# Attention values with the values held still, two groups of heads side by side, and exponentials divided before they are turned

## The chip, the cores and the metric

The kernel runs on one core of a Trainium2 chip. The metric is the device time of one launch in microseconds (us); the time before is the median of three runs. A profile is one further execution of the same kernel, with a span (first to last instruction) and a time of its own.

## What is computed

Two layers over 256 tokens of width 1024. Each layer has a mixer and then a feed-forward part: layer 0 a dense SwiGLU, layer 1 a top-2-of-8 expert SwiGLU; a last RMSNorm ends it. The change lies in the attention half of the mixers:

```python
scores = einsum('bnqkgd,bnskd->bnkgqs', qb, kb) * (HEAD_DIM ** -0.5)   # 8 query heads, 2 key/value heads, head_dim 64
m = maximum(max(where(valid, scores, NEG_INF)), sink_b)
p = exp(scores - m)
denom = sum(p) + exp(sink_b - m)
out = einsum('bnkgqs,bnskd->bnqkgd', p / denom, vb)
y_att = rmsnorm(out, att_out_g);  y_conv = rmsnorm(short_conv(bg, cg, u, conv_w), conv_out_g)
return concatenate([y_att, y_conv], axis=-1) @ w_out
```

With 256 tokens every query block of 128 sees both key blocks, so a head has 128x256 scores for each of the two query tiles (t = 0 and 1). Query heads 0 to 3 use the first key/value head, 4 to 7 the second.

## The kernel before

The order of each engine's work is written out by hand; the engines meet only at semaphores, and each works through its own queue in order. Line numbers are those of the profile.

**Weights in pieces.** The projections run at full float32 accuracy by splitting both sides in a high and a low part. A weight piece is 128x1024: ScalarE copies the high part (L809), VectorE subtracts it (L1213, the low part), TensorE then does three products (L1897 to L1899) for each 128x512 output. Pieces live in a ring of 6. In a mixer they are numbered 0 to 25: q 0 to 3, kv 4 and 5, c 6 to 9, u 10 to 13, b 14 to 17, out0 18 to 21, out1 22 to 25. The loads are issued on SyncE's queue. `OUT_ORDER` makes the output projection take the four conv blocks (k = 4 to 7) first and the four attention blocks (k = 0 to 3) last.

**The attention of one tile t.** TensorE computes the scores of 8 heads in 4 banks of two heads (L1956). VectorE masks a bank (L1314), takes the row maximum (L1316) and its negative (L1317); ScalarE then makes the two exponentials of the bank with their sums (L886), after the fourth bank also that of the sink (L890). TensorE transposes the 16 blocks of exponentials (`turn_probs`, L1968) into the same banks; ScalarE and VectorE copy two banks each to `probT` (L809, L1330). `values` (L1978) holds a block of `probT` (128x128) as weights and streams 64 columns of v, 16 products for a tile, each of which is two records in the trace. VectorE divides the outcome by the denominators (`attended`, L1335).

**Around it.** The exponentials of tile 0 are turned between pieces u3 and b0; values of tile 0 come after piece b3, then `turn_probs` of tile 1, the transposes of the conv gate (L2021), values of tile 1, and the output projection. After its first piece TensorE transposes the attended values of both tiles (L2039), ScalarE and VectorE make their high and low parts (L809, L1404). VectorE's queue behind the scores of tile 1 is: the conv (L1377, L1381), `attended` of tile 0, the copies of `probT`, the product with the gate (L1391), the low parts of the conv blocks (L1396, for which ScalarE's high parts come first), the sums of squares (L1400).

Of the kernel before, what the change touches and what calls it, by code (L numbers as in the profile page):

```python
# [25 lines left out]
ALU = mybir.AluOpType  # L26
# [34 lines left out]
             ("out0", 4, 1, 2), ("out1", 4, 2, 2)]  # L61
# [269 lines left out]
CONSTS = 7  # L331
# [3 lines left out]
def build_trunk(nc, x_d, pos_d, mix_g, w_in, conv_w, sink, att_g, conv_g, w_out, ffn_g, dg, du, dd,  # L335
                router, eg, eu, ed, final_g, out_d):
    ctx = ExitStack()
    with ctx:
# [163 lines left out]
        def e_at(s, g):  # L502
# [21 lines left out]
        att = qT.rearrange("p c n -> p (c n)").rearrange("p (t n) -> p t n", t=NT)  # L524
# [4 lines left out]
        sq_sum = silu[:, 0, :]  # L529

# [23 lines left out]
        av_done, att_done, attss_done, attms_done, attstd_done, attn_done = (  # L554
            sem("av_done"), sem("att_done"), sem("attss_done"), sem("attms_done"), sem("attstd_done"), sem("attn_done"))
# [3 lines left out]
        attT_done, mixhi_done, mixlo_done = sem("attT_done"), sem("mixhi_done"), sem("mixlo_done")  # L559
# [75 lines left out]
        w_out_v = w_out.rearrange("l (h p k) n -> l h p k n", h=2, k=4)  # L635
# [10 lines left out]
        def _(sp):  # L646
# [3 lines left out]
            def mixer_loads(layer):  # L650
# [4 lines left out]
                for name, _, buf, _ in MIX_UNITS:  # L655
# [26 lines left out]
            def dense_down(j):  # L682
                if j < 2:

                    sp.wait_ge(mixlo_done, 8)
# [71 lines left out]
        def _(pool):  # L757
# [13 lines left out]
            nc.gpsimd.dma_start(g_att[:, :, :], att_g.rearrange("l (p k) -> p l k", k=4)).then_inc(consts_in, 16)  # L771
# [26 lines left out]

            nc.gpsimd.dma_start(rout[:, :, 0:NE], router[0].rearrange("(k p) e -> p k e", k=KT)).then_inc(router_in, 16)
# [7 lines left out]
        def _(act):  # L807
# [73 lines left out]
            def exps(layer, t):  # L881
# [7 lines left out]
                act.wait_ge(sinkd_done, 2 * layer + t + 1)  # L889
                nc.scalar.activation(esink[:, t, :], sinkd[:, t, :], ACT.Exp).then_inc(exp_done, 1)  # L890

            def probT_copy(layer, t):
                act.wait_ge(probT_done, 2 * layer + t + 1)
                for b in range(2):
                    copy(probT[:, b * 512:(b + 1) * 512], bank[b][:, :]).then_inc(probT_out_a, 1)

            def mixer(layer):
# [53 lines left out]
                act.wait_ge(yc_done, layer + 1)  # L951
                for k in range(CT):
                    copy(act_hi[:, 4 + k, :], yc[:, k, :], scale=g_conv[:, layer, k:k + 1]).then_inc(mixhi_done, 1)
                nc.scalar.activation(sq, yc, ACT.Square).then_inc(sq_done, 1)
                nc.scalar.activation(table_warm[:, :], eps[:, :], ACT.Sqrt)
                pieces(22, 24)
                for t in range(NT):
                    act.wait_ge(att_done, 2 * layer + t + 1)
                    nc.scalar.activation(prob[:, t * 512:(t + 1) * 512],
                                         att[:, t, :], ACT.Square,  # L960
                                         accum_out=ss_a[:, t:t + 1]).then_inc(attss_done, 1)
                act.wait_ge(attT_done, layer + 1)
                for k in range(4):
                    copy(act_hi[:, k, :], bank[k // 2][:, (k % 2) * 256:(k % 2) * 256 + 256],
                         scale=g_att[:, layer, k:k + 1]).then_inc(mixhi_done, 1)
                act.wait_ge(attss_done, 2 * (layer + 1))
                nc.scalar.activation(std_a[:, :], ss_a[:, :], ACT.Sqrt, bias=eps[:, 0:1],
                                     scale=1.0 / AW).then_inc(attstd_done, 1)
                act.wait_ge(cms_done, layer + 1)
                nc.scalar.activation(std_c[:, :], bank[CMS][:, 0:NT], ACT.Sqrt, bias=eps[:, 0:1],  # L970
# [223 lines left out]
        def _(dve):  # L1194
# [110 lines left out]

            def masked_scores(layer, t):
# [12 lines left out]
                dve.wait_ge(masked_done, 4 * (i + 1))  # L1319
                v.tensor_tensor(sinkd[:, t, :], sink_sb[:, layer, :], nmx[:, t, :], ALU.add).then_inc(sinkd_done, 1)  # L1320

            def denominators(layer, t):
                dve.wait_ge(exp_done, (NH + 1) * (2 * layer + t + 1))
                link(v.tensor_tensor(den[:, t, :], psums[:, t, :], esink[:, t, :], ALU.add))
                v.reciprocal(rden[:, t, :], den[:, t, :]).then_inc(rden_done, 1)

            def probT_copy(layer, t):
                dve.wait_ge(probT_done, 2 * layer + t + 1)
# [3 lines left out]
            def attended(layer, t):  # L1332
                dve.wait_ge(av_done, 2 * layer + t + 1)
                dve.wait_ge(rden_done, 2 * layer + t + 1)
                v.tensor_tensor(att[:, t, :].rearrange("p (h d) -> p h d", h=NH),  # L1335
                                bank[6 + t][:, :].rearrange("p (h d) -> p h d", h=NH),
# [1193 lines left out]
```

## Time and profile before

| what | value |
|---|---|
| median of 3 runs | 1269.55 us (1269.49 to 1270.73) |
| profiled execution, its own time | 1270.25 us |
| its span | 1268.5 us |
| TensorE busy | 1241.0 us (98%) |
| VectorE busy | 579.1 us (46%) |
| ScalarE busy | 435.6 us (34%) |
| granted TensorE clock, mean | 0.996 |

The difference of 1.75 us between span and time lies around the span. The first mixer lies between 0 and about 104 us, the dense part up to 292 us, the second mixer up to about 391 us, the experts after that. TensorE's busy time is modelled, since matmuls overlap: what an operation costs in a row is read from the start of one row to the start of the next.

### The profile page before, as it was taken

Reading aid. Unit: us, or ns where it says so; the run is one execution under the profiler, and the core shown is the slowest. Engines: PE = TensorE matmul, PEld = TensorE weight load, DVE = VectorE, ACT = ScalarE, POOL = GpSimd, SP = SyncE. Lnnn points to the kernel's source line nnn. Section 1 sums busy time; section 2 is a strip of 40 time slices with the busy share of each in tenths; the row PEclk is TensorE's granted clock in tenths of the full one; section 3 lists DMA queues with packets and bytes.
Section 4 is the critical chain, followed back from the end, with each engine's and each line's share of the span. In section 5 each row is a group of like instructions: output and inputs, shape, how many; then the busy total and the mean of one; then the engine's idle time right before and its main releaser. Section 6 shows DMA issues by size and latency. Waiting matters only on the chain.

```text
span 1268.5 us, 31549 instructions
## 1 busy us (share of the span) xinstructions
PE 1241.0 (98%) x14347; PEld 966.9 (76%) x14347; DVE 579.1 (46%) x944; ACT 435.6 (34%) x678; POOL 11.8 (1%) x35
## 2 busy tenths in 40 slices
PE   7999999999998999999999999999999999999997
PEld 6888888888887677777767778766677778768894
DVE  5786555556687556565765656421100112210003
ACT  6664444446554454354643545200000000000002
POOL 3000000000000000000000000000000000000000
PEclk9999999999998999999999999999999999999999
DMA  9345844165005999999999999999999999999993
GB/s 345 139 154 221 315 161 172 70 234 195 5 1 218 420 421 426 419 421 420 421 425 421 420 421 420 422 423 419 420 414 421 397 397 399 413 419 421 423 421 133
DMA packets 109018, 419.50 MB, mean 331 GB/s; under 512 B 4632, under 2 KB 8768, under 8 KB 100688
## 3 DMA queue, kind: packets, MB, share of 16 engines
q1 hardware_dynamic: 107776, 416.30, 81.0%
q8 instruction: 115, 1.88, 0.5%
q0 software_dynamic: 544, 1.12, 0.3%
q14 instruction: 23, 0.19, 0.0%
q10 hardware_dynamic: 560, 0.01, 0.0%
HBM read 416.37 MB, written 1.05 MB: 329 GB/s over the span
## 4 chain that ended last, share of the span: by engine, by line
PE 85%; DMA 11%; DVE 2%; ACT 1%; SPq 1%; issue 1%; DVEq 0%; ACTq 0%
PE bank L2281 25%; PE bank L1897 13%; PE bank L1898 13%; PE bank L1899 13%; PE bank L2345 12%; DMA ring<-in_moe_w_down 6%; DMA ring_after<-in_moe_w_down 2%; DMA ring<-in_moe_w_up 2%; PE bank L2216 2%; PE bank L2210 2%; PE bank L1978 1%; ACT w_hi L809 1%; SPq L723 1%; PE bank L1956 1%; DVE w_lo L1668 1%; PE bank L1968 1%
## 5 line engine op out<-in xcount | busy, mean ns | idle before, releaser
L1668 DVE TENSOR_TENSOR w_lo<-ring,w_hi 128x896 fp32r<-128x896 f32 (+2 forms) x192 | 202.1, 1089 | 80.3 <-ACT w_hi L809 74.5
L2281 PE MATMUL bank<-ring,late_acts 128*32 128x224 f32 x4736 | 234.0, 353 | 0.0
L2281 PEld LDWEIGHTS bank<-ring,late_acts 128*32 128x32 f32 x4736 | 188.9, 110 | 40.9 <-issue 5.0
L809 ACT ACTIVATE w_hi<-ring 128x896 fp32r<-128x896 f32 (+2 forms) x192 | 176.0, 948 | 117.7 <-PE bank L1899 72.8
L1083 ACT ACTIVATE silu_buf<-bank 128x224 f32<-128x224 f32 (+2 forms) x76 | 29.2, 395 | 433.9 <-PE bank L2281 433.9
L1897 PE MATMUL bank<-hi,act_hi 128*128 128x512 f32 (+1 forms) x400 | 155.3, 388 | 0.8 <-DVE lo L1213 0.8
L1899 PE MATMUL bank<-hi,act_lo 128*128 128x512 f32 (+1 forms) x400 | 153.2, 383 | 0.0
L1898 PE MATMUL bank<-lo,act_hi 128*128 128x512 f32 (+1 forms) x400 | 153.2, 383 | 0.0
L1213 DVE TENSOR_TENSOR lo<-raw_gu,hi 128x1024 fp32r<-128x1024 f32 x96 | 113.5, 1222 | 39.9 <-ACT hi L809 39.6
L1691 DVE TENSOR_TENSOR silu_buf<-silu_buf,bank 128x224 f32<-128x224 f32 (+2 forms) x76 | 32.0, 435 | 207.3 <-PE bank L2281 186.0
L809 ACT ACTIVATE hi<-raw_gu 128x1024 fp32r<-128x1024 f32 x96 | 97.5, 1061 | 40.4 <-PE bank L1899 35.7
L2281 PE MATMUL bank<-ring,first_acts 128*32 128x224 f32 x2048 | 104.3, 354 | 0.6 <-ACT silu_buf L1083 0.6
L1897 PE MATMUL bank<-w_hi,wide_hi 128*128 128x512 f32 (+1 forms) x256 | 94.9, 371 | 0.9 <-ACT silu_buf L1083 0.8
L1898 PE MATMUL bank<-w_lo,wide_hi 128*128 128x512 f32 (+1 forms) x256 | 94.0, 367 | 0.0
L1899 PE MATMUL bank<-w_hi,wide_lo 128*128 128x512 f32 (+1 forms) x256 | 93.8, 366 | 0.0
L2345 PE MATMUL bank<-ring,at_buf 128*32 128x256 f32 x1456 | 85.8, 380 | 3.3 <-DMA ring<-in_moe_w_down 3.3
L2281 PEld LDWEIGHTS bank<-ring,first_acts 128*32 128x32 f32 x2048 | 63.6, 110 | 33.0 <-issue 5.1
L1897 PEld LDWEIGHTS bank<-hi,act_hi 128*128 128x128 f32 x400 | 75.8, 190 | 16.1 <-DVE lo L1213 1.2
L1899 PEld LDWEIGHTS bank<-hi,act_lo 128*128 128x128 f32 x400 | 75.6, 189 | 14.9
L1898 PEld LDWEIGHTS bank<-lo,act_hi 128*128 128x128 f32 x400 | 75.9, 190 | 14.0
L2345 PEld LDWEIGHTS bank<-ring,at_buf 128*32 128x32 f32 x1456 | 51.5, 110 | 33.5 <-DMA ring<-in_moe_w_down 4.7
L1897 PEld LDWEIGHTS bank<-w_hi,wide_hi 128*128 128x128 f32 x256 | 48.0, 188 | 10.9 <-DVE w_lo L1668 3.1
(257 smaller groups left out, 1340.2 us busy)
## 6 DMA issues: line engine op xcount, KB each, us to landing
ring<-in_moe_w_up SPq DMA_DIRECT2D x59, 1792.0 KB, 20.3
ring<-in_moe_w_gate SPq DMA_DIRECT2D x58, 1792.0 KB, 20.2
ring<-in_moe_w_down SPq DMA_DIRECT2D x53, 1792.0 KB, 20.4
ring_after<-in_moe_w_down SPq DMA_DIRECT2D x11, 1792.0 KB, 19.7
raw_gu<-in_w_in SPq DMA_DIRECT2D x7, 2048.0 KB, 12.3
raw_gu<-in_dense_w_gate SPq DMA_DIRECT2D x5, 2048.0 KB, 7.9
raw_gu<-in_dense_w_up SPq DMA_DIRECT2D x5, 2048.0 KB, 12.5
raw_d<-in_dense_w_down SPq DMA_DIRECT2D x5, 2048.0 KB, 14.5
```

The costliest lines, as they stand in the source:

```text
L809: return nc.scalar.activation(out, in_, ACT.Copy, **kw)
L1083: nc.scalar.activation(out, gate, ACT.Silu).then_inc(e_silu_done, 1)
L1213: v.tensor_tensor(out, src, h, ALU.subtract).then_inc(lo_done, 1)
L1668: v.tensor_tensor(w_lo[:, n % WP, 0:b - a], flat(u)[:, a:b], w_hi[:, n % WP, 0:b - a], ALU.subtract).then_inc(w_lo_done, 1)
L1691: v.tensor_tensor(gated_e, gated_e, up, ALU.mult).then_inc(e_gated_done, 1)
L1897: mm(out, ah, wh, start=start, stop=False, **kw)
L1898: mm(out, ah, wl, start=False, stop=False, **kw)
L1899: return mm(out, al, wh, start=False, stop=stop, **kw)
L2210: ins = mm(bank[b][:, i * m:(i + 1) * m], xn[:, t, k * P:(k + 1) * P], sel[:, t, 0:m], start=t == 0, stop=t == 1)
L2216: return mm(bank[b][:, :], gselT[0:m, tile, t * P:(t + 1) * P], yt[0:m, tile, c * 512:(c + 1) * 512], start=start, stop=stop)
L2281: ins = mm(bank[b][32 * c:32 * c + 32, 0:n], acts[STEPS[s][0]][:, k, g.col:g.col + 32], w[:, c], start=k == 0, stop=k == KT - 1)
L2345: ins = mm(bank[g.acc][32 * c:32 * c + 32, g.acc_col:g.acc_col + 256], e_at(s, g)[:, 32 * f:32 * f + 32], flat(u)[:, at:at + 256], start=o ...
```

## The change

`values` swaps the roles: 64 columns of v are held as weights and the transposed probabilities of four heads (128x512) are streamed, one key/value head to output partitions 0 to 63 and the other to 64 to 127. That is 4 products a tile in place of 16. Their output has the head dimension on the partitions already, so the transposes of the attended values go, and so does the division by denominators on it; the rows of w_out and of the gain are loaded in the matching order. The division moves ahead: VectorE multiplies each head's exponentials in place by the reciprocal denominator, in two batches of four heads within `masked_scores`, each behind the score bank that follows. `turn_probs` now waits for these (`probs_done`). Tile 0 is turned one piece later, behind b0. The four copies of `probT` of tile 1 are all ScalarE's. The high and low parts of attention are made tile by tile right from the banks of `values`; the sum of squares goes over the partitions with two further small products. In the diff `denominators`, `masked_scores` and `attended` are VectorE's, `probT_copy` is ScalarE's (VectorE's own is called for tile 0 only), the functions from `turn_probs` on are TensorE's, and the last piece is of SyncE's loads.

```diff
+            def denominators(layer, t, c):
+                i = 2 * (2 * layer + t) + c
+                dve.wait_ge(exp_done, 5 * (i + 1))
+                link(v.tensor_tensor(batch(den, t, c), batch(psums, t, c), batch(esink, t, c), ALU.add))
+                link(v.reciprocal(batch(rden, t, c), batch(den, t, c)))
+                for b in SCORE_BANKS[2 * c:2 * c + 2]:
+                    for h in (2 * b, 2 * b + 1):
+                        own = prob[:, h * SEQ:(h + 1) * SEQ]
+                        v.tensor_scalar(own, own, rden[:, t, h:h + 1], None, ALU.mult).then_inc(probs_done, 1)
...
             def masked_scores(layer, t):
...
+                    if n % 2 == 1:
+                        c = n // 2
+                        dve.wait_ge(masked_done, 4 * i + n + 1)
+                        v.tensor_tensor(batch(sinkd, t, c), batch(sink_sb, layer, c), batch(nmx, t, c),
+                                        ALU.add).then_inc(sinkd_done, 1)
+                    if n >= 2:
+                        denominators(layer, t, n - 2)
...
+            def attended(layer, t):
...
+                dve.wait_ge(attss_done, i + 1)
+                for k in range(4):
+                    v.scalar_tensor_tensor(out=act_lo[:, k, tt], in0=bank[6 + t][:, k * P:(k + 1) * P],
+                                           scalar=g_att[:, layer, k:k + 1], in1=act_hi[:, k, tt],
+                                           op0=ALU.mult, op1=ALU.subtract).then_inc(attlo_done, 1)
+                v.tensor_reduce(asq_sum[:, tt], prob[:, t * 512:(t + 1) * 512].rearrange("p (k q) -> p q k", k=4),
+                                AX, ALU.add).then_inc(asq_summed, 1)
...
             def probT_copy(layer, t):
                 act.wait_ge(probT_done, 2 * layer + t + 1)
-                for b in range(2):
+                for b in range(2 if t == 0 else 4):
                     copy(probT[:, b * 512:(b + 1) * 512], bank[b][:, :]).then_inc(probT_out_a, 1)
...
             def turn_probs(layer, t):
                 for n, b in enumerate(SCORE_BANKS):
-                    pe.wait_ge(exp_done, (NH + 1) * (2 * layer + t) + 2 * n + 2)
+                    pe.wait_ge(probs_done, NH * (2 * layer + t) + 2 * n + 2)
...
             def values(layer, t):
-                for h in range(NH):
-                    g = AW + KVW + HD * (h // (NH // NKV))
-                    for kt in range(NT):
-                        ins = mm(bank[6 + t][:, h * HD:(h + 1) * HD], probT[:, h * 256 + kt * P:h * 256 + kt * P + P],
-                                 qkv[:, kt, g:g + HD], start=kt == 0, stop=kt == 1)
+                for kt in range(NT):
+                    for g in range(NKV):
+                        c = AW + KVW + HD * g
+                        four = probT[:, 1024 * g:1024 * g + 1024].rearrange("p (h k q) -> p k h q", h=4, k=NT)
+                        ins = mm(bank[6 + t][HD * g:HD * g + HD, :], qkv[:, kt, c:c + HD], four[:, kt],
+                                 start=kt == 0, stop=kt == 1)
...
                 scores(layer, 0)
                 mix_pieces(layer, "u", (6, 7), 2, 4)
-                turn_probs(layer, 0)
                 pe.wait_ge(c_out, 2 * (layer + 1))
-                mix_pieces(layer, "b", (4, 5), 0, 2)
+                mix_pieces(layer, "b", (4, 5), 0, 1)
+                turn_probs(layer, 0)
+                mix_pieces(layer, "b", (4, 5), 1, 2)
...
                 values(layer, 1)
-                out_pieces(layer, 0, 0, 1)
-                pe.wait_ge(att_done, 2 * (layer + 1))
-                for k in range(4):
-                    for t in range(NT):
-                        c = (k % 2) * 256 + t * P
-                        ins = tr(bank[k // 2][:, c:c + P], att[:, t, k:AW:4], ident[:, :])
-                ins.then_inc(attT_done, 1)
-                out_pieces(layer, 0, 1, 2)
+                out_pieces(layer, 0, 0, 3)
...
+                pe.wait_ge(asq_summed, 2 * (layer + 1))
...
-                out_pieces(layer, 0, 2, 4)
+                out_pieces(layer, 0, 3, 4)
...
-                        for h in range(2):
-                            sp.dma_start(unit[buf][:, 4 * h:4 * h + 4, :],
-                                         w_out_v[layer, h, :, :, c * 512:(c + 1) * 512]).then_inc(unit_in[buf], 16)
+                        cc = slice(c * 512, (c + 1) * 512)
+                        sp.dma_start(unit[buf][:, 4:8, :], w_out_conv[layer, :, :, cc]).then_inc(unit_in[buf], 16)
+                        for g in range(NKV):
+                            sp.dma_start(unit[buf][HD * g:HD * g + HD, 0:4, :], w_out_att[layer, g, :, :, cc])\
+                                .then_inc(unit_in[buf], 16)
```

VectorE, tile 1 of the first mixer, before (`bank` holds scores, `mx` and `nmx` their maxima, `den` and `rden` the denominators of tile 0, `y` the conv):

```order
L1324 TENSOR_TENSOR den<-psums,esink 128x8
L1325 RECIPROCAL rden<-den 128x8
L1213 TENSOR_TENSOR lo<-raw_gu,hi 128x1024 x4
L1314 TENSOR_TENSOR bank<-bank,mask 128x2x128
...
L1320 TENSOR_TENSOR sinkd<-sink_sb,nmx 128x8
L1377 TENSOR_SCALAR y<-raw_d,cw 128x256 x4
L1381 SCALAR_TENSOR_TENSOR y<-raw_d,cw,y 128x256 x8
L1335 TENSOR_TENSOR raw_d<-bank,rden 128x512
L1330 COPY raw_d<-bank 128x512 x2
L1324 TENSOR_TENSOR den<-psums,esink 128x8
L1325 RECIPROCAL rden<-den 128x8
L1391 TENSOR_TENSOR y<-y,bank 128x512 x2
```

The same stretch of VectorE's queue now, from the third score bank of tile 1 on:

```order
L1327 TENSOR_TENSOR den<-psums,esink 128x2x2
L1328 RECIPROCAL rden<-den 128x2x2
L1332 TENSOR_SCALAR raw_d<-raw_d,rden 128x256 x4
L1342 TENSOR_TENSOR bank<-bank,mask 128x2x128
L1344 TENSOR_REDUCE mx<-bank 128x2
L1345 SCALAR_TENSOR_TENSOR nmx<-mx,nsink 128x2
L1350 TENSOR_TENSOR sinkd<-sink_sb,nmx 128x2x2
L1327 TENSOR_TENSOR den<-psums,esink 128x2x2
L1328 RECIPROCAL rden<-den 128x2x2
L1332 TENSOR_SCALAR raw_d<-raw_d,rden 128x256 x4
L1409 TENSOR_SCALAR y<-raw_d,cw 128x256 x4
L1413 SCALAR_TENSOR_TENSOR y<-raw_d,cw,y 128x256 x8
```

The denominators came behind the conv and the copies; they, with eight multiplications on the exponentials (`raw_d`), now stand among the score banks and ahead of the conv.

TensorE, from the values of tile 0 on, before:

```order
L1978 MATMUL bank<-raw_d 128x64 x16
L1968 MATMUL bank<-ident,raw_d 128x128 x16
L2021 MATMUL bank<-ident,xn 128x128 x8
L1978 MATMUL bank<-raw_d 128x64 x16
L1897 MATMUL bank<-hi,act_hi 128x512
```

And the same place now:

```order
L2008 MATMUL bank<-raw_d 64x512 x4
L1998 MATMUL bank<-ident,raw_d 128x128 x16
L2052 MATMUL bank<-ident,xn 128x128 x8
L2008 MATMUL bank<-raw_d 64x512 x4
L1920 MATMUL bank<-hi,act_hi 128x512
```

The order is the same; the values have 4 products of 512 columns for 16 of 64.

## Rows read from the trace of the kernel before

**Rows 1.** Timeline of TensorE: start us, us, line, output and inputs, count [idle before].

```profile
61.77 2.00 PE L1956 MATMUL bank<-raw_d 64*128 64x256 f32 x16
...
70.25 3.68 PE L1978 MATMUL bank<-raw_d 128*128 128x64 f32 x32
73.77 1.92 PE L1968 MATMUL bank<-ident,raw_d 128*128 128x128 f32 x16
...
77.16 3.75 PE L1978 MATMUL bank<-raw_d 128*128 128x64 f32 x32 [0.51 <-DVE raw_d L1330]
80.72 0.48 PE L1897 MATMUL bank<-hi,act_hi 128*128 128x512 f32 x1
...
83.58 1.12 PE L2039 MATMUL bank<-ident,raw_d 128*128 128x128 f32 x8
84.45 0.48 PE L1897 MATMUL bank<-hi,act_hi 128*128 128x512 f32 x1
...
87.29 0.50 PE L2046 MATMUL bank<-ones,silu 128*128 128x1 f32 x4
```

**Rows 2.** Timeline of VectorE, both mixers.

```profile
48.09 0.43 DVE L1314 TENSOR_TENSOR bank<-bank,mask 128x256 f32<-128x256 f32 x1 [2.05 <-PE bank L1956]
...
49.36 0.42 DVE L1314 TENSOR_TENSOR bank<-bank,mask 128x256 f32<-128x256 f32 x1
...
53.08 0.16 DVE L1317 SCALAR_TENSOR_TENSOR nmx<-mx,nsink 128x2 f32<-128x2 f32 x1
...
55.38 2.36 DVE L1213 TENSOR_TENSOR lo<-raw_gu,hi 128x1024 fp32r<-128x1024 f32 x2 [1.93 <-ACT hi L809]
...
60.17 0.16 DVE L1324 TENSOR_TENSOR den<-psums,esink 128x8 f32<-128x8 f32 x1
...
60.48 4.58 DVE L1213 TENSOR_TENSOR lo<-raw_gu,hi 128x1024 fp32r<-128x1024 f32 x4
64.98 0.42 DVE L1314 TENSOR_TENSOR bank<-bank,mask 128x256 f32<-128x256 f32 x1
...
70.23 1.14 DVE L1377 TENSOR_SCALAR y<-raw_d,cw 128x256 f32<-128x256 f32 x4
...
77.24 1.24 DVE L1391 TENSOR_TENSOR y<-y,bank 128x512 f32<-128x512 f32 x2
79.14 1.68 DVE L1396 SCALAR_TENSOR_TENSOR act_lo<-y,g_conv,act_hi 128x256 fp32r<-128x256 f32 x4 [0.66 <-ACT act_hi L809]
...
81.56 2.01 DVE L1400 TENSOR_REDUCE silu<-gated 128x256 f32<-128x1024 f32 x1
...
105.20 0.61 DVE L1239 SCALAR_TENSOR_TENSOR act_lo<-bank,g_ffn,act_hi 128x128 fp32r<-128x128 f32 x2
...
346.85 0.42 DVE L1314 TENSOR_TENSOR bank<-bank,mask 128x256 f32<-128x256 f32 x1
```

**Rows 3.** Timeline of ScalarE, first mixer.

```profile
53.27 0.48 ACT L886 ACTIVATE raw_d<-bank,nmx 128x256 f32<-128x256 f32 x1 [0.24 <-DVE nmx L1317]
...
54.19 0.21 ACT L890 ACTIVATE esink<-sinkd 128x8 f32<-128x8 f32 x1
...
75.72 1.08 ACT L809 ACTIVATE raw_d<-bank 128x512 f32<-128x512 f32 x2 [3.30 <-PE bank L1968]
78.59 1.71 ACT L809 ACTIVATE act_hi<-y,g_conv 128x256 fp32r<-128x256 f32 x4 [1.78 <-DVE y L1391]
```

**Rows 4.** Timeline of SyncE's DMA queue, the loads of w_out.

```profile
21.83 11.91 SPq L666 DMA_DIRECT2D raw_gu<-in_w_out  x4
```

**Rows 5.** Timeline of TensorE in the experts, 32 output rows at a time.

```profile
431.08 1.72 PE L2281 MATMUL bank<-ring,first_acts 128*32 128x224 f32 x32
```

**Rows 6.** Stretches: us; busy PE, PEld, DVE, ACT, POOL; clock; DMA share; GB/s.

```profile
396.00:398.00 2.00, 1.34 (x4) 1.34 (x5) 1.83 (x12) 0.00 (x0) 0.00 (x0) 0.50 0.93 268
398.00:400.00 2.00, 2.00 (x7) 2.00 (x7) 0.64 (x3) 0.37 (x2) 0.00 (x0) 0.50 1.04 403
400.00:402.00 2.00, 2.00 (x12) 2.00 (x12) 1.38 (x2) 1.52 (x6) 0.00 (x0) 0.85 1.00 383
```

More of the change, by code:

```diff
@@ L330 @@
 FIRST_BANKS = (3, 4, 6, 7)
-CONSTS = 7
+CONSTS = 6
 POOL_STEPS = 7 + NE + 5
@@ L529, in build_trunk, with batch @@
         sq_sum = silu[:, 0, :]
+        asq_sum = silu[:, 1, :]
+        def batch(a, t, c):
+            return a[:, t, :].rearrange("p (g c i) -> p c g i", g=NKV, c=2)[:, c]
         unit_in = [sem(f"unit_in{n}") for n in range(4)]
@@ L634, in build_trunk @@
         w_in_v = w_in.rearrange("l (p k) n -> l p k n", k=KT)
-        w_out_v = w_out.rearrange("l (h p k) n -> l h p k n", h=2, k=4)
+        w_out_att = w_out[:, 0:AW].rearrange("l (g k d) n -> l g d k n", g=NKV, k=4)
+        w_out_conv = w_out[:, AW:D].rearrange("l (p k) n -> l p k n", k=CT)
         dg_v = dg.rearrange("l (p k) n -> l p k n", k=KT)
@@ L797, in _ @@
             assert n == POOL_STEPS
+            for layer in range(2):
+                for g in range(NKV):
+                    nc.gpsimd.dma_start(g_att[HD * g:HD * g + HD, layer, :],
+                                        att_g[layer, 256 * g:256 * g + 256].rearrange("(k d) -> d k", k=4),
+                                        allow_slow_non_contiguous=True).then_inc(att_gain_in, 16)
             nc.gpsimd.dma_start(rout[:, :, 0:NE], router[0].rearrange("(k p) e -> p k e", k=KT)).then_inc(router_in, 16)
@@ L1318, in masked_scores, with probT_copy @@
                                            in1=nsink[:, layer, two], op0=ALU.mult, op1=ALU.min).then_inc(masked_done, 1)
[L1319 to L1328, printed above, removed]
+                    if n % 2 == 1:
+                        c = n // 2
[4 more added lines that the diff above has]
+                        denominators(layer, t, n - 2)
+            def probT_copy(layer):
+                dve.wait_ge(probT_done, 2 * layer + 1)
                 for b in range(2, 4):
@@ L1332, in attended @@
             def attended(layer, t):
[L1333 to L1336, printed above, removed]
-                                rden[:, t, :].unsqueeze(2).to_broadcast([P, NH, HD]), ALU.mult).then_inc(att_done, 1)
+                i = 2 * layer + t
+                dve.wait_ge(attss_done, i + 1)
+                tt = slice(t * P, (t + 1) * P)
+                for k in range(4):
+                    v.scalar_tensor_tensor(out=act_lo[:, k, tt], in0=bank[6 + t][:, k * P:(k + 1) * P],
[3 more added lines that the diff above has]
+                                AX, ALU.add).then_inc(asq_summed, 1)
             def mixer(layer):
@@ L1370, in mixer @@
                                            in1=z[:, t, :], op0=ALU.mult, op1=ALU.mult).then_inc(z_done, 1)
-                denominators(layer, 0)
                 pieces(18, 22)
@@ L1384, in mixer @@
                     link(ins)
-                attended(layer, 0)
-                probT_copy(layer, 1)
-                denominators(layer, 1)
                 dve.wait_ge(bT_done, layer + 1)
@@ L2044, in mixer @@
                 pe.wait_ge(sq_summed, layer + 1)
-                for t in range(NT):
-                    ins = mm(bank[CMS][:, t:t + 1], sq_sum[:, t * P:(t + 1) * P], ones[:, 0:1], start=True, stop=True)
+                pe.wait_ge(asq_summed, 2 * (layer + 1))
+                for i, sums in enumerate((sq_sum, asq_sum)):
+                    for t in range(NT):
+                        c = i * NT + t
+                        ins = mm(bank[CMS][:, c:c + 1], sums[:, t * P:(t + 1) * P], ones[:, 0:1], start=True, stop=True)
                 ins.then_inc(cms_done, 1)
-                out_pieces(layer, 0, 2, 4)
+                out_pieces(layer, 0, 3, 4)
                 pe.wait_ge(cstd_done, layer + 1)
```

84 lines of the change are left out of this document (41 added, 43 removed).

## Prediction

> **What bounds the kernel now.** I read the page's shares first, then TensorE's timeline through both mixers, then what VectorE and ScalarE do beside it. TensorE is busy 98% of the span, and in the changed part of the first mixer its one pause is 0.51 us, ahead of the values of tile 1 [rows 1]. So TensorE's own instructions are the path there. The second mixer repeats the first 281.9 us later: the masking of tile 1 starts at 346.85 for 64.98 [rows 2]. What saves TensorE time is worth its full length, as long as what TensorE waits for is ready. VectorE's slack is therefore the question. The output projection starts at 80.72; the first conv low part that it needs is started at 79.14 and takes a quarter of 1.68 us, so it is there at about 79.6 [rows 1, 2]: a slack of only 1.1 us. Upstream VectorE has one pause, 1.93 us, behind the scores of tile 0 [rows 2].
>
> **What TensorE saves.** Values of a tile cost 73.77 - 70.25 = 3.52 us and 80.72 - 77.16 = 3.56 us [rows 1]: 32 records at 0.11 us for 64 columns each. The new form has 4 products, 8 records, of 512 columns. No row has that shape, so by the nearest ones: the scores are 16 records of 256 columns, with two halves of the array at once, in 2.00 us [rows 1]; 8 records of 512 columns are the same number of columns, so about 2.0 us. In the experts 32 records of 224 columns that use a quarter of the output columns take 1.72 us [rows 5]: 7168 column steps in 1.72 us, 0.24 ns each, while the scores have 4096 in 2.00 us, 0.49 ns. With two halves side by side 4096 steps are 2.0 us; with none, twice that, 4.0 us. I take 2.0 (the scores' row is the nearest) and keep 4.0. The saving is 1.5 us a tile. The eight transposes of the attended values also go, 84.45 - 83.58 = 0.87 us, and two more products with `ones` come, about 0.3 us from the 0.50 us of four records [rows 1]. Were that all, and the 0.51 us pause too, TensorE would be 3.52 + 3.56 - 4.0 + 0.87 + 0.51 - 0.3 = 4.2 us shorter in each mixer.
>
> The Trainium skill (TensorEngine Tiling, Key Properties) says that a change of the tiling mode drains the array. The old values form has no such change and the new one has two a tile; the rows of the scores, which have it on both sides, hold that price in their 2.00 us, so my term does not grow by the rule.
>
> **What VectorE gets.** For each tile: eight multiplications of 128x256 in place and two batches of denominators. The nearest row to a multiplication is L1377, same form, same shape, SBUF to SBUF: four in 1.14 us, 0.285 each [rows 2]. The bounds: 0.42 us, the pitch of the two-input form at that shape (1.68 / 4, L1396), and 0.19 us, close to what the tiny operations take (0.16, L1324) [rows 2]. I take 0.285. A batch of denominators is 0.31 us from the row at 60.17 to 60.48, with one more completion to wait for about 0.4. A batch is 0.4 + 4 x 0.285 = 1.55 us, 3.1 us a tile.
>
> *Tile 0.* Masking a bank is 49.36 - 48.09 = 1.27 us. Three banks from 48.09 end at 52.0 (with the sink subtraction), the first batch at 53.55, the fourth bank at 54.8. From the start of the negative maximum to the end of the sink's exponential is 54.40 - 53.08 = 1.32 us [rows 2, 3], so the second batch may start at 56.1 and ends at 57.7. VectorE then does the two low parts that it started at 55.38: 2.3 us, to 60.0; the copies and z, which before filled the queue from there (55.38 + 2.3 = 57.7) to 60.17, 2.5 us, to 62.5; four low parts, 4.5 us, to 67.05. Masking of tile 1 starts there and not at 64.98: 2.1 us later. The pause of 1.93 us has hidden part of the 3.1, and the denominators that went with 0.3 the rest. TensorE isn't hurt: with b0 (2.7 us) moved ahead, it comes to the turning of tile 0 at about 57.2, and the last heads are ready at 57.8, while the first eight transposes take 0.9 us.
>
> *Tile 1.* Three banks from 67.05: 70.95. First batch: 72.5. Fourth bank: 73.8, with its negative maximum started at 73.7. Exponentials and sink: 75.0. Second batch: 75.1 to 76.7. TensorE, 1.5 us earlier after the new values, stands at `turn_probs` at 72.25, turns the first half, and waits for the second from about 73.2 to 76.2. It ends at about 77.4; before, it was 73.77 + 1.92 = 75.7 [rows 1].
>
> *Copies.* ScalarE makes all four: two took 1.08 us [rows 3], so four take 2.0, from 77.5 to 79.5. Values of tile 1 start at 79.6 for 77.16, and end at 81.6. Behind them on VectorE the conv and its gate: `attended`, copies and denominators are gone from between, so the gate comes right behind the conv: four operations of 0.285 and eight of 0.42 are 4.5 us, with the waits between them 4.6, so it starts at 76.7 + 4.6 = 81.3. Its first half is done 0.62 us later, ScalarE's high part 0.5 us after that, the low part 0.45 us on, with the hand-overs at 83.05 (before, the row at 79.14 came 1.9 us after the gate at 77.24 [rows 2]; the gate now signals by halves, which gains 0.6). The output projection starts at 83.05, not 80.72: **2.3 us later**.
>
> *After that.* TensorE has 0.87 us less (no transposes) and 0.3 more (`ones`). The third output piece needs the attention low parts of tile 1. VectorE: conv low parts to 84.4, sum of squares 2.0 us [rows 2] from 84.8 to 86.8, four low parts of tile 0 at 0.30 (L1239: two in 0.61 [rows 2]) and a reduction of half the former size, 1.0 us: 89.0; the first low part of tile 1 at about 89.2. TensorE is there at 83.05 + 5.6 = 88.6: 0.5 us of wait. Net for the mixer: 2.3 - 0.87 + 0.3 + 0.5 = 2.2 us longer.
>
> *At nothing.* The w_out loads become three where two were; they are issued from 21.83 on for 11.91 us [rows 4], and their first low part is made after 60.48 [rows 2], more than 25 us later. The gain is loaded by four small DMAs on GpSimd's queue at its start, and needed after 80 us. The dense weights wait for low parts that shift by some 2 to 5 us; they are used much later.
>
> **Sum.** 2 mixers x 2.2 = 4.4 us. Nothing behind them is tied to a fixed time: the expert loads start when the routing is known. From the profiled execution's own 1270.25 us that is 1274.65; the median of the runs lies 0.7 below that execution, so **1274.0 us** in their terms.
>
> **The range of the likeliest case.** With 0.42 us a multiplication, 8 x 0.135 = 1.1 us more stands in the chain of tile 1 and 0.9 in that of tile 0: 2 us a mixer, 1278. With 0.19, 0.095 x 16 = 1.5 less each: 1271. With values at 4.0 us, the values of tile 1 end at 83.6 and not 81.6, 0.5 us behind the low parts: 0.5 a mixer, 1275. So 1271 to 1278.
>
> **Rivals.** (A) *VectorE keeps up, TensorE's saving counts.* 2 x 4.2 = 8.4 us off: 1261. For it: TensorE is 98% busy and VectorE only 46%. Against it: the chain above would have to be 4.6 us shorter in each mixer, and most of it are rows of the same engine in order. It decides where the last heads of tile 1 are scaled before about 73 us.
>
> (B) *TensorE's clock falls in the new pauses.* In the routing TensorE had work in small bits and pauses, and ran at the lower level (1.2 GHz) until after 400 us, although it had worked without pause from about 396.7: 1.34 + 2.00 + 0.6 us of work at half speed [rows 6], so 2.0 us lost. The new pauses of 3.0, 1.3 and 1.4 us stand close together, with 4 us of work among them. One such fall in each mixer, with the output projection behind it, adds up to 2.0 each: 1278. It decides when the pause in `turn_probs` passes about 3 us. The Trainium skill (TensorE: Matmul & The Clock Gate, HAM oscillation) warns that an array left waiting by turns falls back to half rate and pays for getting back; rows 6 show such a fall, but after emptier work than here.
>
> (C) *The slower chain and the savings cancel.* If the multiplications go at 0.19, the output projection starts 2.3 - 1.5 = 0.8 us late; if the attention low parts are then there in time, 0.8 - 0.87 + 0.3 = 0.2 us is left in each mixer: 1270. For it: nothing but one row of another place stands for the multiplications. Against it: that row has their very form.
>
> (D) *The halves don't run side by side.* Then the change doesn't do what it says on TensorE; 1275, since TensorE waits for VectorE anyway.
>
> **Chances.** Likeliest case with D, 1271 to 1278: 0.60. B 0.14. A 0.12. C 0.14. A measurement here tells a difference from about 0.2%, 2.5 us. Faster by more than that is A and a little of C, 0.14; within it the rest of C and the low end of the likeliest, 0.16; slower 0.70. The range from 1268.5 to 1278.5 leaves out A and the far end of B.
>
> **What would show it.** In the profile after: a wait of TensorE in the transposes of tile 1 for VectorE's multiplications, near 3 us, in both mixers; the multiplications at 0.28 to 0.35 us; masking of tile 1 at 67; ScalarE's four copies ending near 79.5; the first output matmul at 83 and its wait put down to the low parts of the conv; values at 2.0 us. I am wrong if the masking of tile 1 starts before 66, if the scaled heads are there before TensorE asks, or if the clock leaves 1.00 in the mixers.

## The result, and the profile after

The changed kernel takes 1273.93 us (median of 9 runs, 1272.79 to 1274.71) against 1270.23 for the one before (9 runs): ratio 1.0032, interval 1.0023 to 1.0041. It is slower, by 3.7 us. The profiled span is 1272.6 us for 1268.5.

The same markers in the two traces show where the 4.1 us of span lie. The first mixer, from the first masking operation of VectorE (48.09 before, 48.48 after) to TensorE's first transposes behind the mixer (104.12, 106.64), goes from 56.03 to 58.16 us. The dense layer behind it stays at 187.90 (to 292.02 and 294.54). The second mixer, to the start of the routing (390.99, 395.52), goes from 98.97 to 100.98. So 2.13 and 2.01 us are lost in the mixers, which is the whole 4.1 us: what is left, the first masking 0.39 us later and a part behind the routing that is 0.43 us shorter, cancels. Positions below are often given from a run's first masking operation, because the profiles start at different moments (it lies between 47.52 and 48.80 us in them).

Timeline of TensorE after, first mixer (start us, us, line, output and inputs, count, idle before and its releaser), answering to rows 1:

```profile
70.73 1.94 PE L2008 MATMUL bank<-raw_d 128*64 128x512 f32 x8
72.60 1.09 PE L1998 MATMUL bank<-ident,raw_d 128*128 128x128 f32 x8
76.33 1.49 PE L1998 MATMUL bank<-ident,raw_d 128*128 128x128 f32 x8 [2.63 <-DVE raw_d L1332]
77.62 1.91 PE L2052 MATMUL bank<-ident,xn 128*128 128x128 f32 x8
79.98 2.16 PE L2008 MATMUL bank<-raw_d 128*64 128x512 f32 x8 [0.45 <-ACT raw_d L824]
83.28 0.47 PE L1920 MATMUL bank<-hi,act_hi 128*128 128x512 f32 x1 [1.15 <-DVE act_lo L1424]
```

The values of tile 0 take 1.87 us (70.73 to 72.60) where they took 3.52. But a hole of 2.63 us stands in the turning of tile 1, and a second one of 1.15 us ahead of the output projection. That starts 34.80 us behind the first masking for 32.63 [rows 1, 2].

Timeline of VectorE after, tile 1 of the same mixer, answering to rows 2:

```profile
67.26 0.43 DVE L1342 TENSOR_TENSOR bank<-bank,mask 128x256 f32<-128x256 f32 x1
...
71.66 1.14 DVE L1332 TENSOR_SCALAR raw_d<-raw_d,rden 128x256 f32<-128x256 f32 x4
...
75.24 0.17 DVE L1327 TENSOR_TENSOR den<-psums,esink 128x4 f32<-128x4 f32 x1 [0.98 <-ACT esink L906]
...
75.66 1.14 DVE L1332 TENSOR_SCALAR raw_d<-raw_d,rden 128x256 f32<-128x256 f32 x4
76.71 1.14 DVE L1409 TENSOR_SCALAR y<-raw_d,cw 128x256 f32<-128x256 f32 x4
77.88 3.38 DVE L1413 SCALAR_TENSOR_TENSOR y<-raw_d,cw,y 128x256 f32<-128x256 f32 x8
81.30 1.29 DVE L1420 TENSOR_TENSOR y<-y,bank 128x512 f32<-128x512 f32 x2
82.65 1.68 DVE L1424 SCALAR_TENSOR_TENSOR act_lo<-y,g_conv,act_hi 128x256 fp32r<-128x256 f32 x4
```

The queue is full from the masking to the low parts of the conv but for one pause behind the sink's exponential. Waits of TensorE in the two mixers (in total, times, longest):

```profile
PE bank L1998 <- DVE raw_d L1332: 5.3, 2, 2.6
PE bank L1920 <- DVE act_lo L1424: 2.0, 2, 1.1
PE bank L2008 <- ACT raw_d L824: 0.9, 2, 0.5
```

And TensorE's clock in the stretches around them (busy PE, its count, granted clock, DMA share, GB/s):

```profile
74.00:76.00 2.00, 0.00 (x0) 1.00 1.05 408
76.00:78.00 2.00, 1.67 (x10) 0.76 1.05 410
78.00:80.00 2.00, 1.55 (x10) 0.50 0.96 369
80.00:82.00 2.00, 2.00 (x8) 0.88 0.00 1
```

The clock fell to its lower level (0.50 is 1.2 GHz) behind the 2.63 us hole. The chain of the page's fourth part says the same of the whole run: VectorE's share is 8% for 2% before, TensorE's 80% for 85%. (That is how much of the chain now runs through VectorE's queue, not how much time was lost.)

### The profile page after: what moved, and what is told of

It is laid out like the page before. It is cut to its first block, busy times and chain, and to the rows that moved or that the text cites. A ratio compares the mean times of both kernels' runs of the same rounds, so it can differ in the third digit from the quotient of the medians.

```text
span 1272.6 us, 31410 instructions
## 1 busy us (share of the span) xinstructions
PE 1238.0 (97%) x14243; PEld 955.4 (75%) x14243; DVE 589.7 (46%) x992; ACT 439.0 (34%) x690; POOL 12.6 (1%) x38
## 3 DMA queue, kind: packets, MB, share of 16 engines
q8 instruction: 114, 1.87, 0.5%
## 4 chain that ended last, share of the span: by engine, by line
PE 80%; DMA 9%; DVE 8%; ACT 1%; issue 1%; SPq 0%; ACTq 0%; DVEq 0%
PE bank L2308 25%; PE bank L2372 13%; PE bank L1920 12%; PE bank L1921 12%; PE bank L1922 12%; DMA ring<-in_moe_w_down 7%; DMA ring_after<-in_moe_w_down 2%; PE bank L2243 2%; PE bank L2237 2%; DVE w_lo L1691 1%; DVE lo L1231 1%; DVE mx L1344 1%; DVE raw_d L1332 1%; DMA raw_gu<-in_w_in 1%; DVE y L1413 0%
```

## The experiments

Theory V: the order of VectorE's queue sets the start of the output projection. Against it stand theory T (TensorE's own new instructions), the clock, and later theory D (the hand-overs between the engines). Each run is told by its time, its ratio to the kernel before, and two positions from the first masking: the start of the output projection ("start", 32.63 before, 34.80 after), and the end of the first mixer ("end", 56.03 and 58.16). The second mixer is 98.97 and 100.98. Each ratio is to the kernel before as it ran beside that experiment: 1269.68 us for the first four, 1269.79 for the next four and 1269.55 for the last four, for 1270.23 in the result. So times of different groups are compared through their ratios and positions first. A position is that of one profiled execution.

**No multiplications in tile 0.**

```
 def denominators(layer, t, c):
     ...
+    if t == 0:
+        v.reciprocal(batch(rden, t, c), batch(den, t, c)).then_inc(probs_done, 4)
+        return
```

> The changed kernel without the eight multiplications of tile 0 in both mixers (the exponentials of tile 0 stay undivided; all waits stay). Theory V (VectorE's queue sets when the output projection starts): most of the 2.3 us of tile 0 is hidden, since behind it VectorE waits for the transposes of tile 0 and for ScalarE's high parts; masking of tile 1 starts about 0.7 us earlier, so about 1.3 us off in all, 1272.6. Theory T (TensorE's own instructions set the time, its waits are small change): no difference, 1273.9.

1271.89 us, ratio 1.0022 (1.0011 to 1.0034); start 34.12, end 57.46. The 2.3 us of multiplications were worth 0.7 in each mixer; without them VectorE waits 0.50 us for ScalarE and 0.88 us for TensorE's turning ahead of its copies. V's number holds: masking of tile 1 starts 18.11 us behind the first masking for 18.78.

**No multiplications in tile 1** (the same edit with `t == 1`).

> The changed kernel without the eight multiplications of tile 1 in both mixers (the exponentials of tile 1 stay undivided; all waits stay). Theory V: all eight stand in the chain to the output projection, 8 x 0.285 = 2.3 us a mixer, so 4.6 us off, 1269.3; TensorE's wait in the transposes of tile 1 falls from 2.6 to about 1.5 us. Theory T: at most the 2.6 us wait counts and what is behind it hides nothing, so under 2 us off in all, 1272 or more.

1269.37 us, ratio 0.9998 (0.9988 to 1.0007); start 32.54, end 55.89. All 2.26 us come back, and TensorE's hole shrinks by 1.71 us:

```profile
74.59 1.09 PE L2001 MATMUL bank<-ident,raw_d 128*128 128x128 f32 x8 [0.92 <-DVE rden L1329]
...
77.83 1.94 PE L2011 MATMUL bank<-raw_d 128*64 128x512 f32 x8 [1.19 <-ACT raw_d L824]
80.99 0.47 PE L1923 MATMUL bank<-hi,act_hi 128*128 128x512 f32 x1 [1.22 <-DVE act_lo L1427]
```

**The values of tile 0 made twice.**

```
-for kt in range(NT):
+for kt in [0, 1] * (2 if t == 0 else 1):
```

> The changed kernel with the products of values of tile 0 made twice (8 products for 4, same outcome), which adds about 1.9 us of TensorE ahead of the transposes of tile 1 in both mixers. Theory V: TensorE waits there for VectorE anyway, nothing changes, 1273.9 within 0.5. Theory T: 1.9 us more in each mixer, 1277.7.

1274.4 us, ratio 1.0035 (1.0022 to 1.0047); start 34.80. TensorE got 1.71 us more work (74.63 - 71.05 for 72.60 - 70.73) and the hole became 1.71 us smaller:

```profile
71.05 3.65 PE L2008 MATMUL bank<-raw_d 128*64 128x512 f32 x16
74.63 1.09 PE L1998 MATMUL bank<-ident,raw_d 128*128 128x128 f32 x8
76.65 1.18 PE L1998 MATMUL bank<-ident,raw_d 128*128 128x128 f32 x8 [0.92 <-DVE raw_d L1332]
```

T falls: what the change saves in TensorE's values of tile 0 is worth nothing.

**Work in the hole,** so that the clock stays up.

```
+if t == 1 and n == 2:
+    for _ in range(11):
+        mm(bank[7][:, :], zeros[:, 0:P], zeros[:, :], start=True, stop=True)
```

> The changed kernel with 11 products of zeros (128x512, 0.23 us each) in TensorE's pause in the transposes of tile 1, into a bank that is free there. Rival C (the fall of TensorE's clock to the lower level behind that pause costs time): the clock stays at the upper level, and 1 to 2 us come off in each mixer, 1270 to 1272. Theory V: the clock stays up, the transposes behind the pause take 0.9 us and not 1.3 to 1.8, but the output projection still waits for the conv's low parts at 83.3; nothing comes off, 1273.9 within 0.5.

1273.56 us, ratio 1.0033 (1.0020 to 1.0045); start 34.80, end 58.16, both as in the changed kernel. The clock stayed at 1.00 and the instructions behind got their full speed:

```profile
72.61 2.78 PE L1996 MATMUL bank<-zeros 128*128 128x512 f32 x11
75.49 1.18 PE L2001 MATMUL bank<-ident,raw_d 128*128 128x128 f32 x8
76.51 1.13 PE L2055 MATMUL bank<-ident,xn 128*128 128x128 f32 x8
78.83 1.94 PE L2011 MATMUL bank<-raw_d 128*64 128x512 f32 x8 [1.19 <-ACT raw_d L824]
82.44 0.47 PE L1920 MATMUL bank<-hi,act_hi 128*128 128x512 f32 x1 [1.68 <-DVE act_lo L1424]
```

(The fall of the clock, rival C of this expectation, is rival B of the prediction.) What they gained, 1.3 us, stands in the two waits, 1.19 for 0.45 and 1.68 for 1.15. In the changed kernel the fall of the clock costs nothing.

**All four copies of tile 0 on ScalarE.**

```
-for b in range(2 if t == 0 else 4):        # ScalarE, behind turn_probs
+for b in range(4):
...
-    probT_copy(layer)                      # VectorE
```

> The changed kernel with all four copies of probT of tile 0 on ScalarE, which idles there; VectorE loses two copies of 0.6 us ahead of the masking of tile 1. Theory V (the queue of VectorE sets the start of the output projection): masking of tile 1 and all behind it 1.2 us earlier in each mixer, 2.4 us off, 1271.5. Theory D (what limits is the number of engine hand-overs, exponentials to sums to transposes to copies, not how much VectorE has in its queue): the hand-overs are the same, no difference, 1273.9.

1273.46 us, ratio 1.0031 (1.0020 to 1.0041); start 34.64. A miss: 0.16 us instead of 1.2, close to the number of theory D. VectorE got its time back and spent it waiting, since ScalarE's copies had pushed its high parts back:

```profile
59.75 1.40 DVE L1396 SCALAR_TENSOR_TENSOR xn<-bank,rstd,xn 128x512 f32<-128x512 f32 x2
62.11 4.63 DVE L1231 TENSOR_TENSOR lo<-raw_gu,hi 128x1024 fp32r<-128x1024 f32 x4 [0.96 <-ACT hi L824]
```

**And the conv's first tap on ScalarE too.**

```
+for k in range(CT):                        # ScalarE
+    copy(yc[:, k, :], zT[:, k, 0:SEQ], scale=cw[:, layer, 0, k:k + 1]).then_inc(tap_done, 1)
...
-for k in range(CT):                        # VectorE
-    ins = v.tensor_scalar(yc[:, k, :], zT[:, k, 0:SEQ], cw[:, layer, 0, k:k + 1], None, ALU.mult)
-link(ins)
+dve.wait_ge(tap_done, CT * (layer + 1))
```

> b1, and the first tap of the conv (four multiplications of 128x256, 1.14 us) from VectorE to ScalarE, ahead of the exponentials of tile 1. Theory V: another 1.1 us earlier at the gate, the output projection starts 2.3 us earlier than in the changed kernel, 4.6 us off in all, 1269.3, about the kernel before. Theory D: the attention's chain is as long as in b1 or 0.4 longer, since the exponentials of the first bank wait for the taps: no better than b1.

1271.04 us, ratio 1.0011 (1.0001 to 1.0020); start 33.49, end 56.84. The tap itself gave its 1.15 us in each mixer, where theory D had nothing. The time is still 1.7 us above the 1269.3 expected, for what the copies had not brought is missing here too. The output projection now starts with no wait, right behind the values.

**GpSimd makes half of the conv** (on the run with the copies on ScalarE; ScalarE makes the first tap of the other half).

```
+for k in (2, 3):                           # GpSimd; taps 1 and 2 likewise, then two additions
+    ins = nc.gpsimd.tensor_scalar(yc[:, k, :], zT[:, k, 0:SEQ], cw[:, layer, 0, k:k + 1], None, ALU.mult)
```

> b1, with the conv of the last two channel blocks wholly on GpSimd and the first tap of the first two on ScalarE. VectorE keeps four operations of 0.42 of the twelve. Theory V: its part of the gate could start 2.8 us earlier than in b1, but then the values of tile 1 are what ends last (masking of tile 1 is no earlier than in b1): they end about 80.8 on the scale of the changed kernel's profile, so the projection starts 2.5 us earlier than there; 5 to 5.5 us off, 1268.6. Theory D: as b1.

1275.18 us, ratio 1.0039 (1.0025 to 1.0053); start 34.71. A miss by 6.6 us. The profile explains only part of it: the profiled execution was the shortest of the five (1272.95 us, the longest 1275.92), and in it the mixers take 57.58 and 100.43 us, some 0.6 us less each than in the changed kernel, where about 2.6 was expected. What made the other executions longer is in no profile. First the timeline of GpSimd, then that of VectorE beside it:

```profile
66.51 2.28 POOL L822 TENSOR_SCALAR y<-raw_d,cw 128x256 f32<-128x256 f32 x2 [53.18 <-ACT raw_d L849]
68.89 3.77 POOL L828 TENSOR_SCALAR gated<-raw_d,cw 128x256 f32<-128x256 f32 x4
72.74 2.94 POOL L835 TENSOR_TENSOR y<-y,gated 128x256 f32<-128x256 f32 x4
```

```profile
71.50 2.11 DVE L1363 TENSOR_SCALAR raw_d<-raw_d,rden 128x256 f32<-128x256 f32 x4
73.53 0.42 DVE L1373 TENSOR_TENSOR bank<-bank,mask 128x256 f32<-128x256 f32 x1
...
75.05 0.65 DVE L1381 TENSOR_TENSOR sinkd<-sink_sb,nmx 128x4 f32<-128x4 f32 x1
76.20 0.16 DVE L1358 TENSOR_TENSOR den<-psums,esink 128x4 f32<-128x4 f32 x1 [0.50 <-ACT esink L931]
...
76.61 1.14 DVE L1363 TENSOR_SCALAR raw_d<-raw_d,rden 128x256 f32<-128x256 f32 x4
```

The four multiplications that ran beside GpSimd took 2.11 us, those behind it 1.14. They are on the chain that feeds the hole, which is 2.96 us here; so is the sink's subtraction (`sinkd`), 0.65 for 0.16.

**Two of w_out's low parts moved behind the conv's** (on the run above).

```
-pieces(18, 22)                             # ahead of tile 1's masking
+pieces(18, 20)
...
+pieces(20, 21)                             # behind act_lo of the conv
...
-pieces(22, 24)
+pieces(21, 24)                             # behind `attended`
```

> g1, with the low parts of pieces 20 and 21 (the third and fourth of out0) moved behind the conv's low parts on VectorE: masking of tile 1 starts 2.3 us earlier again. Theory V: values of tile 1 end about 2 us earlier than in g1, the projection starts 4.5 us earlier than in the changed kernel, and about 1 us comes back as a wait in the third piece, where the attention's low parts and piece 20 are late: 3.5 to 4 us a mixer, 7 to 8 off, 1266.5, faster than both kernels. Theory D: the attention's chain is set by its hand-overs; masking early doesn't help, as g1.

1273.5 us, ratio 1.0031 (1.0020 to 1.0042), a miss by 7 us. The start moved to 32.89, 1.9 us earlier than in the changed kernel where 4.5 were expected, but the mixer's end is at 58.86. The loads of the dense gate and up weights wait for 22 low parts. SyncE issued them at 89.50 and 90.11, for 67.37 and 67.98 in the changed kernel, and ScalarE sat without its pieces:

```profile
102.61 2.01 ACT L849 ACTIVATE hi<-raw_gu 128x1024 fp32r<-128x1024 f32 x2 [9.75 <-issue]
```

VectorE's low parts of them stand ahead of its update of `x`, for which TensorE then waited 2.50 us. The dense layer took 189.31 us for 187.90. The second mixer, which has no dense layer behind it, took 98.22 us, 2.8 less than in the changed kernel.

These two misses changed several things at once. The last four runs leave GpSimd out and take the rest apart; what GpSimd's share costs in time was not tried by itself.

**The first tap alone on ScalarE** (copies two and two as in the changed kernel).

> The changed kernel, but ScalarE makes the convolution's first tap (four copies of 128x512 with a scale) beside its other work, in place of VectorE's four multiplications of 128x512 by the tap, 0.28 us each, 1.14 us in all, in each of the two mixers; the four copies of the probabilities stay two and two. Theory V (VectorE's queue sets the output projection's start): masking of tile 1 comes no earlier, but the low parts of the convolution come 1.14 us earlier, and the output projection starts just as the values of tile 1 end, about 1.1 us earlier: 1273.9 - 2 x 1.14 = 1271.6 us. Theory D (the hand-overs between TensorE, ScalarE and VectorE set it, not the sum of VectorE's work): no change, 1273.9 us.

1271.83 us, ratio 1.0015 (1.0006 to 1.0024). The time is the one expected from V, but not in the way expected: start 34.80, unmoved, end 57.65, and the second mixer 99.76. So 0.51 us came in the first mixer, where the third output piece no longer waits for the attention's low parts, and 1.22 in the second. The TensorE rows of the first say why, with its clock at 0.66, 0.50, 0.50 and 0.63 in the four stretches from 74 to 82 us:

```profile
75.37 1.97 PE L2002 MATMUL bank<-ident,raw_d 128*128 128x128 f32 x8 [2.62 <-DVE raw_d L1338]
77.13 1.91 PE L2056 MATMUL bank<-ident,xn 128*128 128x128 f32 x8
79.49 2.90 PE L2012 MATMUL bank<-raw_d 128*64 128x512 f32 x8 [0.45 <-ACT raw_d L825]
82.32 0.50 PE L1924 MATMUL bank<-hi,act_hi 128*128 128x512 f32 x1
```

In the second mixer the clock stayed at 1.00 behind a hole of the same length, and the same values took 1.94; the output projection started 33.54 us behind that mixer's first masking, for 34.72 in the changed kernel. In the first the wait for the low parts of the conv is gone, so the slow clock is on the path: it ate 0.7 us of the mixer.

**Two low parts later, the loads kept in their places.**

```
+# first tap on ScalarE, pieces(18, 20), (20, 21), (21, 24) as above
 # SyncE, loads of the dense gate (w = 0) and up (w = 1)
-sp.wait_ge(lo_done, base + [MIX_FIRST["out1"], MIX_PIECES][j])
+sp.wait_ge(lo_done, base + [MIX_FIRST["out0"], MIX_PIECES][j])
...
+if j == 0 and w == 1:
+    sp.wait_ge(lo_done, base + MIX_FIRST["out1"])
```

> The kernel with the first tap on ScalarE, and on VectorE the low parts of two of the output projection's four weight pieces moved behind the low parts of the convolution's result, one of them behind those of the attention. The load of the dense gate's weights no longer waits for all 22 low parts but for the first of the output projection's, the load of the up weights for the later ones, so that both keep their places in time. Theory V: about 2.3 us of low parts leave the way of the masking of tile 1 in each mixer; the output projection then waits for the values instead; my sum gives 2.5 us less for each mixer than in the changed kernel: about 1269 us. Theory D: 1271.6 us or more. If the order of two loads matters, as in the run before this one where they were issued 22 us later, this one must not show ScalarE waiting 9.8 us for the dense pieces.

1270.71 us, ratio 1.0004 (0.9995 to 1.0013); start 32.55, end 56.42, second mixer 99.28. The start came 2.25 us earlier; the mixer gained only 1.7, for the time is 1.7 us above what I expected. The attention's low parts, ahead of which one of the two moved ones now stands, are waited for 1.7 us over both mixers. The loads did not quite keep their places: the gate's was issued at 59.88 us, for 67.37 in the changed kernel, and the up load at 89.91. The late one did no harm, since the gate's was early.

**The attention's low parts ahead of the sums of squares.**

```
-dve.wait_ge(attss_done, i + 1)             # `attended`
+dve.wait_ge(atthi_done, i + 1)
...
+# ScalarE: high parts of both tiles, then sq, then both Squares behind attlo_done
+# VectorE: attended 0, 1; then the reduction of sq, then those of the attention
```

> The kernel before this one, and behind the convolution the low parts of the attention's values of both tiles come ahead of the sums of squares of both (ScalarE makes the high parts of both tiles first and the squares after, VectorE reduces the squares last). The waits of TensorE for those low parts (2.0 us of waits over two mixers for the first, 0.5 us for the second) go. Theory V: another 1 us for each mixer: about 1267 us, less than the kernel before the change. Theory D: as the run above, 1269 us or more; the reductions that now come last would be waited for at the end of the mixer.

1269.09 us, ratio 0.9993 (0.9984 to 1.0002); start 32.54, end 55.67, second mixer 98.50. This is 4.8 us less than the changed kernel and the best of those that do the whole work. It cannot be told from the kernel before. In its two mixers, by the profile, it is 0.4 and 0.5 us shorter than that. I expected 1267; over the run above the mixers gained 0.75 and 0.78 us for 1 each, and the rest of the miss is that run's own. The time by itself would fit theory D (1269 or more); what D cannot explain is the start, 2.26 us earlier, and the gain of the tap. What TensorE still waits for in both:

```profile
PE bank L2014 <- DVE raw_d L1343: 3.1, 2, 1.6
PE bank L2024 <- ACT raw_d L827: 2.4, 2, 1.2
PE bank L1936 <- DVE act_lo L1437: 0.9, 2, 0.5
```

**The same with the old trigger of the loads.**

> The kernel above with the loads of the dense gate's and up's weights behind all 22 low parts again. The two theories on the stall of the run with moved pieces: if it was the late trigger, the loads are issued some 20 us later again, ScalarE waits about 9.8 us for the first dense piece in the first mixer and TensorE 2.5 us at its end, and the time is about 2.5 us above the kernel above, 1269.5 us; if it was GpSimd's share of the convolution, which is absent here, the time is the same as that of the kernel above.

1275.05 us, ratio 1.0043 (1.0029 to 1.0056). The start is 32.55, as in the run above, but the first mixer ends at 60.41, 4.7 us later. First TensorE's rows there, then ScalarE's, then SyncE's queue:

```profile
107.99 0.49 PE L1906 MATMUL bank<-ident,x 128*128 128x128 f32 x2 [4.58 <-DVE x L1452]
108.31 1.28 PE L1894 MATMUL bank<-ident,x 128*128 128x128 f32 x6
```

```profile
103.82 2.00 ACT L825 ACTIVATE hi<-raw_gu 128x1024 fp32r<-128x1024 f32 x2 [11.98 <-issue]
```

```profile
89.48 0.56 SPq L710 DMA_DIRECT2D raw_gu<-in_dense_w_gate  x1
90.09 0.67 SPq L710 DMA_DIRECT2D raw_gu<-in_dense_w_up  x1
```

The trigger was the cause of the stall, not GpSimd. The size I expected, 2.5 us, was too small: TensorE asked 0.5 us earlier than in the run with GpSimd (55.83 us behind the first masking for 56.36), and ScalarE had its pieces 1.5 us later than there (56.24 for 54.70). Behind the wait the clock fell (0.63 and 0.51 from 108 to 112 us), and the dense layer took 189.42 us and not 187.90. The second mixer, 98.47, is as in the run above.

## Why the prediction was right

The mechanism was right, and the number, 1274.0 for 1273.93, came for the most part by its own steps:

- *VectorE gets 16 more multiplications a mixer, at 0.285 us.* They took 1.14 us for each four, as the conv's row said. The two runs without them give what each half is worth: 0.7 us in tile 0 and 2.26 in tile 1. The guess that part of tile 0's is hidden was right.
- *Masking of tile 1 at 67.05, second batch at 75.1.* Less the 0.39 us by which the profile starts later, it was 66.87 and 74.85.
- *TensorE waits about 3.0 us in the turning of tile 1.* 2.63.
- *Values in about 2.0 us, two halves side by side.* 1.87, and the records start in pairs. Rival D is out.
- *ScalarE's copies end at 79.5, values start at 79.6.* 79.98, less 0.39: 79.6.
- *The output projection starts at 83.05, 2.3 us later.* 82.89, 2.17 later from the first masking, and its wait is put down to the conv's low parts.
- *Third piece waits 0.5, the products with `ones` add 0.3, and the mixer loses 2.2 us.* The profile names 0.24 us of wait, but from the start of the output projection to the end of the mixer the run with the tap alone, which doesn't wait there, takes 22.85 us for 23.36: the wait costs 0.5. The `ones` add 0.45 (0.81 for 0.36). The mixers lose 2.13 and 2.01.

That the number is off by less than 0.1 us is luck. The steps gave 4.4 us more than the 1269.55 us of three runs. The nine runs of the result put the kernel before at 1270.23, and against those the change costs 3.7 us (4.1 between the two profiles). A loss forecast 0.7 us too large (0.3 by the profiles) and a starting time 0.7 us too low nearly cancelled.

Rival A, the saving on TensorE, needed VectorE to be ready before 73 us; the values made twice show how little the saving is worth. Rival C needed multiplications of 0.19 us.

One sentence of the prediction was wrong: "I am wrong if ... the clock leaves 1.00 in the mixers". It left, in both, and no step failed with it. Rival B had the mechanism but the wrong price for this place. I let it decide at a pause of about 3 us, and it came at 2.63 (in other runs at 1.93 and 1.96). I priced it at 2.0 us with the output projection behind it; in fact the instructions that ran at the lower level stood in front of two waits, which covered it all. With one of these waits gone it costs 0.7 us. The warning of the Trainium skill (TensorE: Matmul & The Clock Gate, HAM oscillation), that a pausing array falls back and pays for its return, agrees with this trace as to the fall; what was paid here was 0 us, and 0.7 in the run with the tap on ScalarE.

My own repair estimates were worse than the prediction. I counted what left VectorE and not what arrived elsewhere: 0.96 us of late high parts on ScalarE, slower multiplications beside GpSimd, a load behind a count of low parts. What remains of theory D is in the best run: 1.19 us of each mixer are a wait for ScalarE's copies, the same in every mixer of the runs whose clock stayed up there, however VectorE's queue was changed. Whether spreading those copies over two engines in tile 1 would help stays open; it was not tried.

## What to carry to other kernels

A saving on the busiest engine is worth its length only if the instructions that feed it do not grow: here 1.65 us a tile left TensorE, 2.3 us a tile went to a VectorE that is busy 46% of the run but has only one gap, of 0.98 us, in this stretch, and the second decided. When work is moved later in a queue, look for every count that it raises, since a DMA far away may be waiting for that number. And price a fall of TensorE's clock by what ends last behind it, since the same fall cost 0 us under a wait and 0.7 us without it.

## What the runs showed of the hardware

- TensorE's clock fell to 0.50 behind a pause of 2.63 us, and also behind 2.47 us (both runs with the copies on ScalarE and no GpSimd), 1.96 (no multiplications in tile 0) and 1.93 (two low parts later, with GpSimd). It stayed at 1.00 when 2.78 us of products on zeros filled most of the pause, and in the runs where that pause was 0.92 us (no multiplications in tile 1, values twice) or 1.56 us (the last three). But the second mixers of two runs kept 1.00 behind pauses of 1.81 us (two low parts later, with GpSimd) and 2.62 us (the tap alone on ScalarE). How long the lower level lasted varied too: to before 80 us in the run with copies and tap on ScalarE, where the values took 1.94 us, past 80 in the one with the tap alone, where they took 2.90. So the pause's length alone does not settle what a fall costs.
- Two column halves of the array side by side: 8 records of 512 columns in 1.87 us. They start in pairs: two records lie within 0.01 us of each other at 70.73, the next two at 71.21, and each takes 0.59 to 0.64 us.
- Four of VectorE's multiplications from SBUF to SBUF took 2.11 us beside GpSimd and 1.14 alone, while its masking in PSUM kept 0.42. The Trainium skill (SBUF — State Buffer, SBUF: two separate sides) says that the two engines lock one pair of ports for a whole instruction, the other being blocked; on VectorE's side this holds for its two-port modes, and for operations with two SBUF inputs beside a GpSimd instruction that reads SBUF. These rows agree as to which instructions become slower, the subtraction of two small SBUF operands (0.65 for 0.16 at 75.05 us) among them. But an earlier one of the same form, at 69.65 us and also beside GpSimd, kept 0.16. In which mode the multiplications ran, and how long one was blocked, no run shows.
- GpSimd, working beside VectorE and with spans that are rough on this engine, needed 1.14 and 0.94 us for a multiplication of 128x256 by a column and 0.74 for an addition, where VectorE needs 0.285 for the first.
